# Column sums through DRAM, first turns in two parts of tokens, and VectorE's sums moved to the end of a turn

## The reference

```python
cs = jax.nn.silu(c)
for i in range(DEPTH):                       # first block
    ada = cs @ w_ada[i] + b_ada[i]           # 1024 x 6144: shifts, scales, gates
    sh1, sc1, g1, sh2, sc2, g2 = [t[:, None, :] for t in jnp.split(ada, 6, axis=-1)]
    u = x * (1.0 + sc1) + sh1
    y = mixer(u)                             # mLSTM, then differential attention
    x = _layer_norm(DEEPNORM_ALPHA * x + (1.0 + g1) * y, ln_g[i, 0], ln_b[i, 0])
    u = x * (1.0 + sc2) + sh2
    y = _conv_ffn(u, f_w_up[i], f_conv_w[i], f_conv_b[i], f_w_down[i])
    x = _layer_norm(DEEPNORM_ALPHA * x + (1.0 + g2) * y, ln_g[i, 1], ln_b[i, 1])
# second block: mod = silu(c_2) @ mod_w[i] + mod_b[i] (and kv_mod_w), rms_norm for _layer_norm,
# x + (1 + gt1) * mixer(h), then x + (1 + gt2) * sq_relu_mlp(h)
```

## Time and profile before

| what | value |
|---|---|
| median of three runs | 3165.83 us |
| profiled execution, first to last instruction | 3166.5 us |
| mean granted TensorE clock | 0.976 of full |
| TensorE, VectorE, ACT, GpSimd busy | 94%, 63%, 34%, 3% |
| DMA, mean | 109 GB/s |

### The profile page before, as it was taken

How to read it: one execution, slowest core, us unless ns; L and a number is a source line. 1 busy time by engine, 2 the same in 40 slices (tenths; PEclk the granted TensorE clock), 3 DMA queues, 4 the chain that set the end, 5 groups by cost and what they waited for, 6 DMA issues and landing times.

```text
span 3166.5 us, 45854 instructions
## 1 busy us (share of the span) xinstructions
PE 2985.3 (94%) x19638; PEld 2434.7 (77%) x19656; DVE 1981.5 (63%) x3051; ACT 1090.8 (34%) x1667; POOL 97.7 (3%) x116
## 2 busy tenths in 40 slices
PE   6998999999988999997999999899999998899999
PEld 5876888887865788884867887678887877778887
DVE  5856897787567896787455777654444255554353
ACT  2334432233156332233333333242223244542122
POOL 0000000000000000000002222000000001000000
PEclk8999999999998999998999999899999999999999
DMA  8751554545530464542210000222322220032232
GB/s 235 187 160 54 180 179 163 183 160 173 189 106 21 153 199 146 200 163 65 95 49 11 13 13 10 103 87 97 103 93 92 83 94 27 8 107 93 94 105 81
DMA packets 236543, 346.08 MB, mean 109 GB/s; under 512 B 19620, under 2 KB 121964, under 8 KB 236340
## 3 DMA queue, kind: packets, MB, share of 16 engines
q1 hardware_dynamic: 221236, 329.63, 32.3%
q10 hardware_dynamic: 15104, 13.52, 1.3%
HBM read 340.97 MB, written 2.15 MB: 108 GB/s over the span
## 4 chain that ended last, share of the span: by engine, by line
PE 80%; DVE 11%; ACT 5%; DMA 2%; issue 1%; SPq 0%; DVEq 0%; ACTq 0%
PE bank L141 79%; DVE w_tiles L150 2%; PE bank L144 2%; DVE w_low L150 1%; DMA first_ada<-in_w_ada 1%; ACT w_high L147 1%; DVE ada_acc L162 1%; DMA weight_ring<-in_d_w_in 1%; DVE w_g L150 1%; ACT w_tiles L147 1%; DVE x_natural L162 1%; ACT L147 1%; ACT stage L147 0%; DVE d_sm L168 0%; DVE x_sm L168 0%
## 5 line engine op out<-in xcount | busy, mean ns | idle before, releaser
L150 DVE TENSOR_TENSOR w_low<-weight_ring,w_high 128x2048 fp32r<-128x2048 f32 (+2 forms) x212 | 463.8, 2188 | 450.4 <-ACT w_high L147 450.4
L147 ACT ACTIVATE w_high<-weight_ring 128x2048 fp32r<-128x2048 f32 (+2 forms) x212 | 388.1, 1831 | 610.4 <-DMA weight_ring<-in_mlp_down 178.9
L141 PE MATMUL bank<-u_high,w_high 128*128 128x512 f32 x1472 | 578.4, 393 | 12.1 <-DVE w_low L150 6.2
L141 PE MATMUL bank<-u_high,w_low 128*128 128x512 f32 x1472 | 574.8, 390 | 0.0
L141 PE MATMUL bank<-u_low,w_high 128*128 128x512 f32 x1472 | 574.6, 390 | 0.0
L141 PE MATMUL bank<-w_high,u_high 128*128 128x512 f32 x896 | 353.3, 394 | 6.8 <-DVE w_low L150 2.5
L141 PE MATMUL bank<-w_low,u_high 128*128 128x512 f32 x896 | 351.1, 392 | 0.0
L141 PE MATMUL bank<-w_high,u_low 128*128 128x512 f32 x896 | 351.0, 392 | 0.0
L141 PEld LDWEIGHTS bank<-u_high,w_high 128*128 128x128 f32 x1472 | 277.5, 189 | 70.6 <-ACT stage L147 7.1
L141 PEld LDWEIGHTS bank<-u_high,w_low 128*128 128x128 f32 x1472 | 277.4, 188 | 58.7
L141 PEld LDWEIGHTS bank<-u_low,w_high 128*128 128x128 f32 x1472 | 277.7, 189 | 57.0
(11 more groups left out here) (411 smaller groups left out, 4362.5 us busy)
## 6 DMA issues: line engine op xcount, KB each, us to landing
ada_ring<-in_mod_w SPq DMA_DIRECT2D x48, 1024.0 KB, 7.5
weight_ring<-in_f_w_up SPq DMA_DIRECT2D x44, 1024.0 KB, 5.1
ada_ring<-in_w_ada SPq DMA_DIRECT2D x40, 1024.0 KB, 7.1
weight_ring<-in_mlp_up SPq DMA_DIRECT2D x32, 1024.0 KB, 5.4
weight_ring<-in_mlp_down SPq DMA_DIRECT2D x32, 1024.0 KB, 5.0
weight_ring<-in_f_w_down SPq DMA_DIRECT2D x24, 768.0 KB, 4.7
weight_ring<-in_m_w_in SPq DMA_DIRECT2D x16, 1024.0 KB, 10.2
weight_ring<-in_d_w_in SPq DMA_DIRECT2D x12, 1024.0 KB, 5.3
```

Source lines behind the costliest of these rows:

```text
L141: return self.e.matmul(out, l, r, start=start, stop=stop, skip_group_check=True)
L147: return self.e.activation(out, in_, f, **kw) if self.live else QUIET
L150: return self.e.tensor_tensor(out, a, b, op) if self.live else QUIET
```

## The change

- **Sums through DRAM.** VectorE accumulates a block in the ring's own memory (first the second half, then the first, `ada_acc` is gone). SyncE stores the sum [128 x 512] to a DRAM buffer, loads it back folded as [128, 4, 128] (`ada_sum`), GpSimd adds the four planes in two instructions, and TensorE sums over partitions in one matmul with four columns of a 0/1 matrix (`pick`), at the end of the *next* turn. The ring's first half may be loaded again only when the store has landed; the second half when it has been read.
- **Order on VectorE.** In the feed-forward up projections and `d_qk` the block's sum and the layer norm's rows stand at the end of a turn, behind its results, and no longer at its head.
- **Norms in two parts.** Behind six norms only token tiles 0 and 1 are transposed before the next linear. Its first turn is done for tokens 0 to 255 and then for 256 to 511 (kind "f": 192 products of 256 columns instead of 96 of 512; kind "t": by token tiles), with the transposes of tiles 2 and 3 among the products of the first part. ACT and VectorE evict and split half tiles; the residual's last turn is written in a new order with its own stage tiles.
- Loads of gate and norm rows, and stores of gates, move to other places of ACT's queue.

```diff
     def sp_ada(self, sp, b):
         w = self.ada_blocks[b][0]
-        for s in range(2):
+        for s in (1, 0):
             if b > len(self.ada_first):
-                sp.wait_ge(self.V, "ada used", b - 1, s)
+                if s:
+                    sp.wait_ge(self.V, "ada used", b - 1)
+                else:
+                    self.sp_sum_out(sp, b - 1)
+                    sp.wait_ge(self.fold_out, b - 1)
...
+    def sp_sum_out(self, sp, b):
+        if b > self.stored_sum:
+            sp.wait_ge(self.V, "ada summed", b)
+            if b - 2 >= len(self.ada_first):
+                sp.wait_ge(self.fold_in, b - 2)
+            sp.dma_start(self.fold_rows[b % 2], self.aring[:, 0, 0:512]).then_inc(*self.fold_out.landed(b))
+            self.stored_sum = b
+
+    def sp_sum_in(self, sp):
+        b = self.stored_sum
+        if b > self.loaded_sum:
+            sp.wait_ge(self.fold_out, b)
+            if b > len(self.ada_first):
+                sp.wait_ge(self.T, "ada", b - 1)
+            src = self.fold_rows[b % 2].rearrange("a n -> (a n)").rearrange("(q p m) -> p q m", q=4, p=P)
+            sp.dma_start(self.asum[:], src).then_inc(*self.fold_in.landed(b))
...
@@ sp_linear: behind each of a turn's first two weight tiles
                 if w >= AHEAD:
                     self.sp_weight(sp, w)
+                self.sp_sum_in(sp)
...
-    def pe_ada(self, pe, b):
-        ...
-        for j in range(4):
-            m = pe.matmul(self.bank[bank][:, j:j + 1], self.aacc[:, j * P:(j + 1) * P], self.ones[:, 0:1], True, True)
+    def pe_ada(self, pe, name, i):
+        if (name, i) in self.takes:
+            ...
+            pe.matmul(self.bank[bank][:, 0:4], self.asum[:, 0, :], self.pick, True, True).then_inc(*self.T.up("ada", b))
...
     def dve_ffn_up(self, v, l, name, off, rows=None):
         f, L = self.f[l], self.lin[name]
         for i in range(L.turns):
-            if rows and i < TT:
-                rows(i)
-            if i < len(L.ada):
-                self.dve_ada(v, L.ada[i])
             for b in range(4):
...
             if i < len(L.ada):
-                self.dve_ada_take(v, L.ada[i])
+                self.dve_ada(v, L.ada[i])
+            if rows and i < TT:
+                rows(i)
+            self.dve_ada_take(v, name, i)
...
+    def pe_first_f(self, pe, L, u, ends, late):
+        for h in range(2):
+            c = slice(HALF * h, HALF * h + HALF)
+            for s in range(2):
+                ...
+                for kt in range(KT):
+                    for n in range(2):
+                        ...
+                        m = self.product(pe, self.bank[bank][:, c], [x[:, w % SLOTS, o:o + P] for x in (self.whigh, self.wlow)],
+                                         [x[:, kt, c] for x in self.u], kt == 0, kt == KT - 1)
+                    if h == 0 and s == 1:
+                        late(kt)
...
+    def pe_turn_late_rows(self, pe, st, src, ready):
+        def late(kt):
+            if kt == 4:
+                self.pe_turn_rows(pe, st, src, ready, 2)
+            if kt == 6:
+                self.pe_turn_rows(pe, st, src, ready, 3)
+        return late
```

More of the change, by code:

```diff
@@ L704, in pe_keep, with pe_linear_f @@
             pe.matmul(self.bank[bank][:], x[:, 0:P], x, True, True)
-    def pe_linear_f(self, pe, name, u, ends):
+    def pe_linear_f(self, pe, name, u, ends, late=None):
         L = self.lin[name]
-        for i in range(L.turns):
+        if late:
+            self.pe_first_f(pe, L, u, ends, late)
+        for i in range(1 if late else 0, L.turns):
             for s in range(2):
@@ L717, in pe_linear_f @@
                         pe.wait_ge(*self.free[bank])
-                    if u:
+                    if u and not late:
                         pe.wait_ge(self.V, "u", u, kt)
@@ L731, in pe_linear_t @@
+    def pe_linear_t(self, pe, name, x, ends, u=None, hidden=None, between=None, beside=None, late=None, ada_early=False):
         L = self.lin[name]
-        for i in range(L.turns):
+        if late:
+            self.pe_first_t(pe, L, u, ends, late)
+            between()
+        for i in range(1 if late else 0, L.turns):
             for q, (k0, nk) in enumerate(L.pieces):
@@ new lines, in act_norm_turn @@
+    def act_norm_turn(self, a, name, st, scale, bias, begun, unit, before=None, loads=None):
+        L = self.lin[name]
+        i = L.turns - 1
+        self.act_ahead_all(a, name, i)
+        begun(0)
+        self.act_ahead(a, name, i, len(L.pieces) - 1)
+        unit(0)
+        begun(1)
+        unit(1)
+        if before:
+            before()
+        self.act_turn_half(a, st, scale, bias, 0)
+        for t in (2, 3):
+            begun(t)
+            unit(t)
+        if loads:
+            loads()
+        self.act_turn_half(a, st, scale, bias, 1)
@@ L884, in dve_residual, with act_residual @@
             self.dve_ahead(v, name, i, len(L.pieces) - 1)
-    def act_residual(self, a, name, follow=None, first=None):
+    def act_residual(self, a, name, follow=None, first=None, turns=None):
         L = self.lin[name]
-        for i in range(L.turns):
+        for i in range(turns or L.turns):
             self.act_ahead_all(a, name, i)
@@ L1687, in pool_diff @@
     def pool_diff(self, g):
+        self.pool_sums(g, "m_out", "f0_up0", "f0_dn0", "f0_up1", "f0_dn1", "d_qk", "d_v")
         self.join(g, self.G, "d heads start")
```

377 lines of the change are left out of this document (259 added, 118 removed).

## The result

The kernel after takes 3404.1 us (median of four runs, 3396.9 to 3408.6), the kernel before 3165.6 beside it; the ratio is 1.0749, with a 95% interval of 1.0736 to 1.0762. It is slower by 239 us. The forecast was 3320, range 3235 to 3365: the direction was right, the size was 84 us short, and the time lies above the range.

The account below looks back on a forecast made before the run. TensorE, busy 94%, was taken to bound the kernel. Feed-forward layers 180 less 2, d_qk 5, clock 8, norms -24 and column sums -12 made +155 on about 3166, so 3320 us, range 3235 to 3365.

Parts of the forecast that it names:

- What bounds, and the queue: TensorE, busy 94%, bounds the kernel; SyncE's in-order queue would hold weight tiles behind the wait for a late sum.
- rival "no stall": Feed-forward turns: no stall at all, only the gains of 29 and 24 stand, 3113 us; chance 0.07.
- The loop, 30.0 us: Feed-forward up projections: blocked turns close at 30.0 us against 22.7, 7.3 lost in each of 14 full loops, 102 us.
- VectorE's 15.1 us: From TensorE's turn start: gate-half convolutions 3.2, second split 2.3, two hidden tiles 1.8 each, next sum 6.1.
- the 14.9 from the sum to the next turn: Chain behind a block's sum: store 2.7, issue 0.45, weight landing 7.5, ACT's high part 1.92, VectorE's low part 2.29.
- d_qk, 1.2 a turn: In d_qk the sum comes about 9 us into the turn, loop 24 us: 1.2 lost, four times, 5 us.
- Norms, -22 and -2: Six norms in two parts save 3.7 us each, 22 us; about 2 more from the clock after the second gap.
- 3.5 us stay, 5.2 for 8.9: Per norm: of an 8.9 us gap, 3.5 of transposes stay; with halved turn and late second part it costs 5.2.
- rival "the norms give nothing": Second part arrives late or half products are slow: 24 us more, 3345; chance 0.12.
- Column sums, -12: Fewer TensorE column-sum matmuls save 0.6 us a block; 20 blocks outside the slowed turns give 12 us.
- Clock, +8: Waits of 12 to 15 us in the down projections bring 1.2 GHz four times: 8 us, bounds 0 and 20.
- rival "the clock stays low": Stalled up turns run two thirds at 1.2 GHz, 36 us per loop, about 3405; chance 0.06.

Follow-up runs that it names:

- four corners: Sums at head or end of a turn, norms whole or in two parts, all with the DRAM fold: 1.0010, 1.0068, 1.0762, 1.0749 against the kernel before.
- the run with d_qk alone: The kernel after with VectorE's sums back at a turn's head in the feed-forward layers, left at the end in d_qk: 1.0132 against the kernel before.
- the run made for it: The kernel before with the 16 squared-ReLU up-projection turns done as 192 products of 256 columns instead of 96 of 512: 1.0124.
- the fold alone: The kernel before with only the column sums changed to the fold through DRAM, sums at a turn's head, norms whole: 1.0010.

## Why the prediction was right in direction and short in size

The mechanism was right, and three terms of the sum had the wrong size. The four corners of the experiments share out 82 of the 84 us that were missing. The sums at a turn's end cost 238 us with the norms whole (1.0762 against 1.0010), where the terms put down for them are 191 (178 for the feed-forward layers, 5 for d_qk, 8 for the clock): 47 short. The norms in two parts gave 4 us for 24: 20 short. The fold cost 3 us where 12 were to be gained: 15 short.

*What bounds, and the queue.* Right. The time went where the forecast said, through the chain it named: SyncE waits for the sum, the weight tile is late, ACT, VectorE, TensorE. Undoing either end of it (VectorE's order, 216 us; SyncE's order, 167) takes most of the loss away. TensorE's turns, 29 to 30 us apart by the forecast, are 31 apart. The rival "no stall" needed a sum 7.1 us into the turn; in the trace it ends 15.1 us in.

*The loop, 30.0 us.* VectorE's 15.1 us were exact, link by link. The failed link is the 14.9 from the sum to the next turn: it is 16.2. The store took 3.5 us, not 2.7: I had taken the landing of a store of twice the size with nothing beside it, while this one is issued 2.4 us behind a 1 MB load. The weight took 7.8 for 7.5. Over the 14 full loops that makes 18 us. In f0_dn0 the store took 6.8, from 570.66 to the next issue at 577.46, and TensorE waited 12.9 for the third piece where the forecast had 11.7:

```profile
588.17 0.79 PE L143 MATMUL bank<-w_high,f_hidden_high 128*128 128x512 f32 x1 [12.91 <-DVE w_low L152]
```

In the other three down projections it waited 9.8, 10.1 and 11.8 for that piece, less than the forecast had. By the marks the four down projections lost 47 us, below their 53 even with the clock's cost in them, and the up projections with the norms ahead of two of them 153, where some 115 were put down. Of these 38, 18 are the loops and 8 the norms; for the remaining 12 no term was found. Together the feed-forward layers lost 200 us where the forecast had 174.

*d_qk, 1.2 a turn.* Wrong, and the largest single miss: 27 us for -1. The loops were 25.8 us in the run with d_qk alone, not 24. One weight tile, issued at 982.33, was with ACT only at 1000.76, 18.4 us later:

```profile
980.94 0.38 ACTq L188 DMA_DIRECT2D d_bias<-bias_rows  x1
...
1000.76 1.91 ACT L149 ACTIVATE w_high<-weight_ring 128x2048 fp32r<-128x2048 f32 x1 [30.87 <-DMA weight_ring<-in_d_w_in]
```

A load of 2 MB from ACT's queue had been issued 1.4 us ahead of it. That this load is what slowed it is read from the rows and not tested. The other half is an omission: d_v has two blocks, its weights are queued behind the sum of d_qk's last turn just as a down projection's third piece is, and the sum of the forecast has no term for it. TensorE waits 14.4 us there.

*Norms, -22 and -2.* Wrong in size. The step is "3.5 us stay, 5.2 for 8.9". The gaps from last to first product:

```profile
1196.72 1.91 PE L146 MATMUL bank<-core_constants,x_natural 128*128 128x128 f32 x16
1199.51 0.36 PE L143 MATMUL bank<-u_high,w_high 128*128 128x256 f32 x1 [0.88 <-DVE u_low L152]
```

Here it is 3.0 us, with 16 transposes in it, as at three of the six; at f0 and d_qk it is 6.4 and 6.2, at g1 4.1, where ACT and VectorE are not through with the first token tiles when the products end. The mean is 4.3 less 0.2, for the 2.5 that I had. The transposes inside the turn were right (1.75). The halving was not: 1.3 us a turn by the count of products and their pace of 0.120, and 2.0 for a whole turn in the run made for it, where I had 0.3. I had extrapolated a pace from two records of another kind of product, half a hundredth of a microsecond off, and 192 of them make the rest. 4.1, 1.75 and 1.3 are 7.1 of the 8.8 that were there, and a second turn that begins 2.4 us late at g1 and a halved turn of 27.2 us for 25.5 at d_qk take more. The rival "the norms give nothing" (chance 0.12) was the true one: 4 us, within the interval of some 8 to either side.

*Column sums, -12.* The saving per turn was a little larger than put down, 0.8 us for 0.6. But what the fold costs was put at nothing. "GpSimd's two additions lie beside other work" is one failed step: VectorE waits for them. The others are the gate columns and the mLSTM layer (9 us by the marks of the fold alone, 5 in the kernel after), where a store lands late behind other traffic and the ring and the weights stand behind it:

```profile
93.78 2.42 SPq L188 DMA_DIRECT2D fold_rows<-ada_ring  x1
110.08 0.37 SPq L188 DMA_DIRECT2D ada_ring<-in_w_ada  x1
110.49 0.51 SPq L188 DMA_DIRECT2D weight_ring<-in_m_w_in  x1
```

*Clock, +8.* The granted clock fell in each stalled turn, for instance at the restart of 723.64 (length, busy, then clock 0.50 of full, that is 1.2 GHz):

```profile
721.30:728.10 6.80, 5.05 (x13) 4.00 (x14) 6.52 (x6) 4.38 (x5) 0.14 (x1) 0.50 0.16 52
728.10:734.90 6.80, 6.80 (x31) 5.62 (x30) 6.45 (x11) 0.78 (x1) 0.00 (x0) 1.00 0.01 2
```

It was at 2.4 GHz again 4.5 us into the products, and TensorE still waited 7.6 us for the next turn's weights. By the rule of the Trainium skill ("TensorE: Matmul & The Clock Gate", "HAM oscillation — how this bites in real kernels") the engine is at the low rate once in every step; the trace agrees, and it cost nothing in these loops because the loop is closed by the others. In the down projections TensorE has no such room, and there the term of 8 us was right: behind the waits for the third piece the low level held another 3.4, 3.2, 5.8 and 3.2 us, with products 0.43 apart for 0.23, which makes some 8 us (an estimate from these rows). The first of the four:

```profile
588.20:591.60 3.40, 3.40 (x8) 2.72 (x9) 3.17 (x5) 1.58 (x2) 1.88 (x2) 0.51 0.16 42
```

The rival "the clock stays low" had about 3405, and 3404 was measured. That is chance: its loops are 36 us, the measured ones 31.3, and most of each turn runs at 2.4 GHz. A comparison of clock levels would have blamed the clock: the mean fell from 0.976 to 0.944.

*The attention heads.* By the marks 6.7 us were lost in the forgetting attention's heads of this one execution, more than the whole last row of the first table. The kernel with sums at the end and norms whole, which has the same heads and as late a start, lost none there, and the kernel in which TensorE adds the planes lost 5.3 there, with an edit that does not touch them. I take it for scatter of that stage; no run was made for it.

## What to carry to other kernels

When work moves within a turn, follow its signal into every in-order queue and write down what stands behind the wait, in every linear that has such a queue and not only where the edit is; then ask of each thing in front of a critical transfer whether that transfer needs it. In this kernel the round trip through DRAM saves TensorE 0.8 us a block and costs time on SyncE's and ACT's queues, GpSimd and VectorE, so it pays only where TensorE is the bound and nothing waits for its landing. Try the parts of a change one at a time: here one gave 0.4% in part of its places, one gave nothing or took 0.6% (by where the sums stand), and one took 7%.

## What the runs showed of the hardware

- GpSimd's additions in SBUF hold up VectorE's operations on SBUF tiles that begin while they run: 1.24 us for 0.68, 0.66 for 0.43, 1.00 for 0.69 on average for the 22 that did, while 15 that had begun before the addition kept their time. GpSimd's pair takes 1.80 for 1.26 beside them. Six convolution steps that read a PSUM bank beside an addition kept their 0.75. The Trainium skill ("SBUF — State Buffer", "SBUF: two separate sides") says that the two engines share a pair of ports and that the one that comes second waits for the whole instruction; the rows agree for VectorE: whether it is slow goes by which of the two began first, and a slow operation ends 0.28 or 0.55 us behind the addition.
- A product of 256 columns in float32 has a pace of 0.120 us, 6% over half of a 512-column product's 0.227, with its weight load as long as itself. A turn in halves takes 23.8 us for 21.8.
- A store of 256 KB from SBUF lands in 3.5 us right behind a 1 MB load, in 6.8 in a down projection, and in 16.3 in the mLSTM layer (issued at 93.78), behind the loads of a weight tile and of half a block. A store of 1024 single values from columns held up ACT for 13.6 us.
